# The inverses of the triangular matrices of a gated delta rule, taken in 64x64 diagonal blocks for two heads at a time

## The reference

```python
def gated_delta_rule(q, k, v, g, beta):
    C = DN_CHUNK
    ...
    decay = jnp.where(causal, jnp.exp(jnp.where(causal, diff, 0.0)), 0.0)
    kb = k * beta[..., None]
    L = jnp.where(strict, jnp.einsum('bhnid,bhnjd->bhnij', kb, k) * decay, 0.0)
    u = lax.linalg.triangular_solve(L, v * beta[..., None], left_side=True,
                                    lower=True, unit_diagonal=True)
    ...
    def step(state, inp):
        qd, kd, u_c, w_c, a_c, gl = inp
        v_new = u_c - jnp.einsum('bhcd,bhde->bhce', w_c, state)
        o = (jnp.einsum('bhcd,bhde->bhce', qd, state)
             + jnp.einsum('bhij,bhje->bhie', a_c, v_new))
        state = state * jnp.exp(gl)[..., None, None] + jnp.einsum('bhcd,bhce->bhde', kd, v_new)
        return state, o
```

## Time and profile before

| | us |
|---|---|
| median of 3 runs | 2665.02 (2660.94 to 2666.0) |
| the profiled execution | 2666.18 |
| its span | 2664.4 |
| PE busy | 2563.9 (96%) |
| DVE, ACT, POOL busy | 1277.0, 1043.9, 1094.7 |

### The profile page before, as it was taken

The page is one execution under the profiler, slowest core; times in us unless marked ns, Lnnn a source line. Parts: engine busy times, 40 slices in busy tenths (PEclk is TensorE's granted clock), DMA queues, the critical chain, the costliest instruction groups (busy, mean ns, idle before and its releaser), DMA issues. The chain is left out here.

```text
span 2664.4 us, 32892 instructions
## 1 busy us (share of the span) xinstructions
PE 2563.9 (96%) x12968; PEld 2094.5 (79%) x12968; DVE 1277.0 (48%) x2116; ACT 1043.9 (39%) x2201; POOL 1094.7 (41%) x815
## 2 busy tenths in 40 slices
PE   7999999999999999999999999999988999899998
PEld 6788887778778888778888877787766788777886
DVE  4667764663341111247777546623375311466453
ACT  5464543443343223254555334433431332323332
POOL 2323223224546555433323232256453555244454
PEclk9999999999999999989999999999998999789999
DMA  3111112112222222121111111123132322272222
GB/s 126 63 48 56 48 40 72 48 55 75 93 71 95 93 91 93 63 87 50 56 48 57 40 64 50 54 87 104 63 105 91 105 95 95 68 210 95 87 95 79
DMA packets 76506, 207.64 MB, mean 78 GB/s; under 512 B 16704, under 2 KB 27712, under 8 KB 75712
## 3 DMA queue, kind: packets, MB, share of 16 engines
q1 hardware_dynamic: 76352, 205.53, 22.7%
HBM read 195.01 MB, written 10.49 MB: 77 GB/s over the span
## 5 line engine op out<-in xcount | busy, mean ns | idle before, releaser
L804 POOL TENSOR_TENSOR wL<-raw,wH 128x512 fp32r<-128x512 f32 x672 | 911.0, 1377 | 1317.4 <-ACT wH L797 1317.0
L822 PE MATMUL ps<-hH,wH 128*128 128x512 f32 (+1 forms) x1664 | 698.2, 420 | 16.2 <-DVE rstdp L1540 4.8
L797 ACT ACTIVATE wH<-raw 128x512 fp32r<-128x512 f32 x672 | 386.8, 624 | 805.2 <-PE ps L824 797.6
L823 PE MATMUL ps<-hL,wH 128*128 128x512 f32 (+1 forms) x1664 | 663.9, 399 | 0.0
L824 PE MATMUL ps<-hH,wL 128*128 128x512 f32 (+1 forms) x1664 | 663.5, 399 | 0.0
L822 PEld LDWEIGHTS ps<-hH,wH 128*128 128x128 f32 (+1 forms) x1664 | 315.2, 189 | 92.3 <-issue 30.6
L824 PEld LDWEIGHTS ps<-hH,wL 128*128 128x128 f32 (+1 forms) x1664 | 314.3, 189 | 78.9 <-issue 2.2
L823 PEld LDWEIGHTS ps<-hL,wH 128*128 128x128 f32 (+1 forms) x1664 | 315.8, 190 | 62.5 <-issue 3.1
L822 PE MATMUL ps<-OH,wH 128*128 128x512 f32 x576 | 235.2, 408 | 7.1 <-issue 4.3
L824 PE MATMUL ps<-OH,wL 128*128 128x512 f32 x576 | 228.8, 397 | 0.0
L823 PE MATMUL ps<-OL,wH 128*128 128x512 f32 x576 | 228.8, 397 | 0.0
(11 more groups left out here) (376 smaller groups left out, 3605.8 us busy)
## 6 DMA issues: line engine op xcount, KB each, us to landing
raw<-w SPq DMA_DIRECT2D x345, 512.0 KB, 3.2
mats<-matsD SPq DMA_DIRECT2D x4, 1408.0 KB, 6.5
x<-xT SPq DMA_DIRECT2D x8, 256.0 KB, 7.8
matsD<-Cd SPq DMA_DIRECT2D x8, 256.0 KB, 2.5
matsD<-wide SPq DMA_DIRECT2D x4, 512.0 KB, 3.5
mats<-lagsD SPq DMA_DIRECT2D x32, 64.0 KB, 6.1
outT<-acc SPq DMA_DIRECT2D x8, 256.0 KB, 2.2
cst<-consts SPq DMA_DIRECT2D x1, 1035.0 KB, 6.8
```

The costliest lines, as they stand in the source:

```text
L797: act.activation(weights_at(slot)[0][:, k, :], raw[:, j % RAW, k, :], ACT.Copy).then_inc(high_done, 1)
L804: pool.tensor_tensor(low[:, k, :], raw[:, j % RAW, k, :], high[:, k, :].bitcast(F32), ALU.subtract).then_inc(low_done, 1)
L822: pe.matmul(out, wh, rH[:, t, :], start=(t == 0), stop=False)
L823: pe.matmul(out, wh, rL[:, t, :], start=False, stop=False)
```

## The change

The inverse is now taken for the two 64x64 diagonal blocks of each chunk, with five levels (b = 2 to 32), and for two heads at a time: `A_GROUPS` is (0, 1), (2, 3), (4, 5), (6), (7). The blocks stand side by side in `XB`, upper and lower 64 partitions holding one block each, 256 columns a head. Every `p` and `q` goes chunk by chunk first to the quarter of PE that has rows 0 to 63 and columns 0 to 63 and then to the one that has rows and columns 64 to 127. Both write into the same PSUM bank, to different partitions. The quarter of the full inverse that couples the two blocks comes from a last step: `turn`, `copy`, `plast`, `copylast`, `qlast`, `negate`. Its three PE stages use one quarter each. `copy` also moves both blocks into `XT` (four ACT instructions for a pair), which D no longer writes.

`LTm` has three buffers. `masked` waits for B of head h-3 and for the group of head h-3. The wait for B of head i-4 moves from tile q to tile k. The constants shrink by 448 columns. A memset of a part of `XT` stands ahead of DVE's first wait in each layer. The table of costs is adapted.

```diff
-LEVELS = (2, 4, 8, 16, 32, 64)
+LEVELS = (2, 4, 8, 16, 32)
+BLK = 64
+A_GROUPS = [(0, 1), (2, 3), (4, 5), (6,), (7,)]
+GROUP_OF = {h: g for g, heads in enumerate(A_GROUPS) for h in heads}
...
-for _name, _n in [("ident", P), ("ones", P), ("upper", P), ("first", P), ("later", P), ("levels", P * len(LEVELS)), ("rot", P),
+for _name, _n in [("ident", P), ("ones", P), ("upper", P), ("first", BLK), ("later", P), ("levels", BLK * len(LEVELS)), ("unit", BLK), ("rot", P),
...
+A_STAGES = (["flipi"] + [f"{s}{v}" for v in range(len(LEVELS))
+                         for s in ["p", "pmask", "q", "update"] + (["flip"] if v < len(LEVELS) - 1 else [])]
+            + ["turn", "copy", "plast", "copylast", "qlast", "negate"])
...
-                if i >= 4:
-                    out.append(last("B", i - 4))
+            if k == "k" and s == "tap3" and i >= 4:
+                out.append(last("B", i - 4))
...
             if s == "masked" and j >= 2:
-                out.append(last("A", j - 2))
                 if j >= 3:
-                    out.append(last("B", j - 3))
+                    out += [last("B", j - 3), last("A", GROUP_OF[j - 3])]
         if kind == "A" and s == "flipi":
-            out.append(last("D", j))
+            out.append(last("D", A_GROUPS[j][-1]))
+        if kind == "A" and s == "copy" and A_GROUPS[j][-1] >= 3:
+            out.append(last("B", A_GROUPS[j][-1] - 3))
         if kind == "B" and s == "v0":
-            out.append(last("A", j))
+            out.append(last("A", GROUP_OF[j]))
...
+                        elif kind == "A" and s == "copy":
+                            heads = A_GROUPS[j]
+                            n = len(heads) * CH
+                            if heads[-1] >= 3:
+                                act.wait_ge(scan_stage, B.end(heads[-1] - 3))
+                            act.wait_ge(inverse_stage, A.before(j, "turn"))
+                            for h in heads:
+                                for b in (lower, upper):
+                                    act.activation(XT[b, h % 3, :, b], XB[b, h % 4, :, :], ACT.Copy)
                             act.wait_ge(inverse_stage, A.before(j, s))
+                            act.activation(Xi[lower, 0:n, :], blocks(psA, 0, heads)[lower], ACT.Copy).then_inc(inverse_stage, 1)
...
                             elif s == "first":
-                                ins = v.tensor_tensor(xt, lt, over_chunks(k_("first")), ALU.mult)
+                                for b in (lower, upper):
+                                    ins = v.tensor_tensor(XB[b, h % 4, :, :], lt[b, :, b], over_chunks(k_("first")[b], CH, BLK), ALU.mult)
                             else:
-                                ins = v.tensor_tensor(xt, over_chunks(k_("ident")), xt, ALU.subtract)
+                                ins = v.tensor_tensor(XB[:, h % 4, :, :], over_chunks(k_("unit")), XB[:, h % 4, :, :], ALU.subtract)
...
+                            if s == "negate":
+                                for i, h in enumerate(heads):
+                                    ins = v.tensor_scalar(XT[lower, h % 3, :, upper], blocks(psA, 1, heads)[lower, i * CH:(i + 1) * CH], -1.0, None,
+                                                          ALU.mult)
...
+                            for i in range(len(A_GROUPS[j]) * CH):
+                                c, lt = i % CH, LTm[A_GROUPS[j][i // CH] % 3]
+                                cc = slice(i * BLK, (i + 1) * BLK)
+                                if s == "turn":
+                                    ins = pe.transpose(psA[lower, 0, cc], xb[lower, i, :], ident[lower, lower])
+                                elif s == "plast":
+                                    ins = pe.matmul(psA[upper, 0, cc], lt[lower, c, upper], Xi[lower, i, :], start=True, stop=True)
+                                elif s == "qlast":
+                                    ins = pe.matmul(psA[lower, 1, cc], Pm[upper, i, :], xb[upper, i, :], start=True, stop=True)
                                 else:
+                                    for b in (lower, upper):
+                                        if s[0] == "p":
+                                            ins = pe.matmul(psA[b, 0, cc], lt[b, c, b], Xi[b, i, :], start=True, stop=True)
+                                        else:
+
+                                            n = LEVELS[int(s[-1])]
+                                            ins = pe.matmul(second_half(psA[b, 1, cc], n), Pm[b, i, :], second_half(xb[b, i, :], n),
+                                                            start=True, stop=True)
```

More of the change, by code:

```diff
@@ L259 @@
 G = Count([(0, G_STAGES)])
-A = Count([(h, A_STAGES) for h in range(HEADS)])
+A = Count([(g, A_STAGES) for g in range(len(A_GROUPS))])
 B = Count([(h, B_STAGES) for h in range(HEADS)])
@@ L314 @@
         ("pe", "D", "sums rows gram turnkv"), ("act", "D", "square ksum root exps copykv"), ("pool", "D", "qdec"),
-        ("pe", "A", "p q turn"), ("act", "A", "copy"),
+        ("pe", "A", "p q turn plast qlast"), ("act", "A", "copy copylast"),
         ("pe", "B", "v o r kv turno"), ("act", "B", "copyv osq square root high"), ("pool", "B", "low"),
@@ L747, in second_half, with over_chunks, blocks, of_group @@
             return m.rearrange("p (b n) -> p b n", n=2 * s)[:, :, s:]
-        def over_chunks(m):
-            return m.unsqueeze(1).to_broadcast([P, CH, P])
+        def over_chunks(m, n=CH, rows=P):
+            return m.unsqueeze(1).to_broadcast([rows, n, BLK])
+        lower, upper = slice(0, BLK), slice(BLK, 2 * BLK)
+        def blocks(m, bank, heads):
+            return m[:, bank, 0:len(heads) * CH * BLK].rearrange("p (c n) -> p c n", n=BLK)
+        def of_group(heads):
+            return XB[:, heads[0] % 4:heads[0] % 4 + len(heads), :, :].rearrange("p h c n -> p (h c) n")
         names = ("loaded0", "loaded1", "loaded2", "high_done", "low_done", "tile_done", "tile_stage",
@@ L1369, in _ @@
                 def _(v):
+                    v.memset(XT[upper, :, :, lower], 0.0)
                     v.wait_ge(params_in, 16)
@@ L1441, in _ @@
                             ins.then_inc(gram_stage, 1)
-                        elif kind == "A" and s[:-1] in ("pmask", "update", "flip"):
+                        elif kind == "A" and (s[:-1] in ("pmask", "update", "flip") or s == "negate"):
+                            heads = A_GROUPS[j]
+                            n = len(heads) * CH
                             if s == "flipi":
-                                v.wait_ge(gram_stage, D.end(j))
+                                v.wait_ge(gram_stage, D.end(heads[-1]))
@@ L1450, in _ @@
                             elif s.startswith("pmask"):
                                 lev = int(s[-1])
-                                m = k_("levels")[:, lev * P:(lev + 1) * P]
-                                ins = v.tensor_tensor(Pm[:, :, :], chunks(psA[:, 0, :]), over_chunks(m), ALU.mult)
+                                m = k_("levels")[:, lev * BLK:(lev + 1) * BLK]
+                                ins = v.tensor_tensor(Pm[:, 0:n, :], blocks(psA, 0, heads), over_chunks(m, n), ALU.mult)
@@ L1693, in _ @@
                             ins.then_inc(gram_stage, 1)
[L1694 to L1702, removed]
-                                else:
-                                    b = LEVELS[int(s[-1])]
-                                    ins = pe.matmul(second_half(psA[:, 1, cc], b), Pm[:, c, :], second_half(XT[:, h % 3, c, :], b),
-                                                    start=True, stop=True)
+                        elif kind == "A" and (s[:-1] in ("p", "q") or s in ("turn", "plast", "qlast")):
+                            pe.wait_ge(inverse_stage, A.before(j, s))
+                            xb = of_group(A_GROUPS[j])
+                            for i in range(len(A_GROUPS[j]) * CH):
[7 more added lines that the diff above has]
+                                    ins = pe.matmul(psA[lower, 1, cc], Pm[upper, i, :], xb[upper, i, :], start=True, stop=True)
+                                else:
+                                    for b in (lower, upper):
[5 more added lines that the diff above has]
+                                                            start=True, stop=True)
```

45 lines of the change are left out of this document (24 added, 21 removed), and 2 rows, old and new, of the table special.

## The result

The changed kernel takes 2754.7 us (median of four runs) against 2665.4: the ratio is 1.034, 95% interval 1.0319 to 1.0361. It is slower by 89 us, where 2629 was forecast. From the page of the kernel after: the span, the engines, and the slices of PE and of its clock, as in the earlier trace rows.

The account below looks back on a forecast made before the run. PE was taken to set the pace in both layers' head stretches. From the profiled 2666.2 us, less 42.6 of PE work and 1 for constants, plus 8 idle, came 2630.6, or 2629 as median; range 2600 to 2678.

Parts of the forecast that it names:

- Prices of the small matmuls: PE's p and q stages: 0.034 us a matmul, 1.31 a pair stage with entry and exit, 0.76 a single; last step 0.06.
- DVE's work to `ga` 0: DVE in the head stretch: flip, mask and update run once per pair, removing 45 of 252 us, less 3 for `negate`.
- D behind `masked`, 5 us: In the loop of pairs: only the end of D, from `masked` on, follows B of an earlier head, 5 us a round.
- the prediction's own sum: Serial chain of A, B and D over layer 0's heads, from D of head 1 at 117 to B of head 7 at 433.
- The gate and its margin of 24 us: First stage of tile `ga` 0 waits for B of head 7, with 24 us to spare before the change, used up after.
- PE's saving of 42.6 us: PE's work on the inverse: 67.3 us a layer against 88.6, so 21.3 less a layer, 42.6 in all.
- 8 us of idle: PE idle time where the loop of pairs and the stream of tiles meet: 4 us a layer, between 0 and 36.
- The loop of pairs decides: Rival: with loaded durations B of head 7 ends at 469, 32 us more a layer than allowed: 2693; chance 0.12.
- The quarters don't overlap: Rival: a matmul in PE's quarter stages costs 0.056, a pair's stage 2.00 us, total 2684; chance 0.11.
- The clock falls: Rival: PE's granted clock drops in the head stretches, eight falls of 5 us a layer, 40 us: 2669; chance 0.04.
- All comes back: Rival: no PE idle time and free entries into the small stages, 2608; chance 0.13.

## Why the prediction was wrong

In the order of its steps, with layer 0's numbers.

**Prices of the small matmuls: right.** A pair stage's 32 matmuls take 1.08 us (1.10 taken), entry 0.32 for 0.33, sixteen of a single head 0.61 (0.55 taken; 150.37 to 150.98 above). The last step was 1.07 us for 16 (169.38 to 170.45 in the last fence below), 0.067 each, where 0.06 was taken. The single heads show most of the sum as time, with one of three tables: 22 us won, where these prices give 27 for eight singles. DVE's work to `ga` 0 fell from 263.0 to 227.4, 36 us where 42 was forecast.

**The loop's term "D behind `masked`, 5 us": the step that failed.** The wait for B of head h-3 stands at three places of D: at `masked`, at `qdec` on POOL and, much earlier, at `qscale`, its first stage on DVE. The list of conditions ahead of the prediction has `masked` alone, and the prediction read the last place. In the kernel before, `qscale` of D 3 starts at 182.9, 12 us after B 0, and of D 7 at 347.5, 16 after B 4, so this wait was met when it came and no row of waits shows it; only the code does. With the pairs it isn't met, and nearly all of D comes behind B: 26, 26 and 23 us in the three rounds of a layer, not 5. With 26 put into the prediction's own sum, up to D 7:

117 + 42 + 33 + 26 + 42 + 33 + 26 + 42 + 33 + 26 = 420.

Measured: 423.4. The other terms were off in ways that cancel: D 1 ended at 127.0, not 117 (the levels of A 0 left PE, but D 1 isn't earlier for it; why isn't settled), A took 46 to 50 instead of 42, B 25 or 26 instead of 33. The kernel with the later wait shows some 10 us a round of the term by itself. It doesn't bring all back, since 13 to 15 us of D stay behind B.

**The gate and its margin of 24 us: wrong too, and independently.** The prediction took `ga` 0 to follow B 7 with 24 us to spare. It stood 24 us behind B 7 before and stands 24 behind it now (480.6 and 504.4), which looks like a gate and isn't one: with D's later wait it comes 14.7 us behind B 7 (458.2 and 472.9). Like `scale` of tile `swq` 0, `rotk` of tile `swk` waits for D 7, which the list ahead of the prediction leaves out. `swv` and the eight `swq` lie between `swk` and `ga` 0. In the fourteen kernels, before and after among them, `ga` 0 comes 77.7 to 83.8 us after D 7 ended, while D 7's end itself goes from 359.4 to 496.0. Before, `rotk` of `swk` ran 0.7 us after the end of D 7 (374.42 and 373.70), and PE was full from there on. So there was no margin against D 7 in the stream of tiles: 423.35 + 81.08 = 504.43. From 420 the prediction's sum would have said 500. Against 453.9 that is 46 a layer, 92 in all, less 1 at the start: 2756 for the median, where 2754.7 was measured. The part that agrees so well is partly luck, by the terms that cancel.

**PE's saving of 42.6 us: right as work, worth nothing as time.** With the chain in charge, 21 us less work a layer is only 21 us more idle. The prediction added the saving to the sum and 8 us of idle beside it, when the loop should have been asked first.

**The rivals.** "The loop of pairs decides" was the mechanism, with D 7 for B 7 as its last member and the price of D left out: 2693 for 2754.7. "The quarters don't overlap": refuted. (The 0.66 us that spoke against it is a row's own length, to be set beside 1.06 and not 0.90; that makes the argument stronger.) "The clock falls": it does, to 0.91 over the stretch, but in the old arithmetic under pair waits as well (0.88), so that the small stages aren't needed for it. How much of A's 47 us is due to it stays open. "All comes back", 2608: no kernel came near it; the best, with all heads single, took 2643.5.

**What was read wrongly.** Full PE and idle 5 us of 380 say that PE sets the pace of this order of work. They don't say how long the serial chain is that would take over, and the margins of that chain were 11 to 16 us at `qscale` of heads 3 to 7 and none at D 7.

## What to carry to other kernels

Before joining two units of a pipelined serial chain into one, write down all waits between its stages, the met ones too, at the first place where each stands, and add the chain up from release to release; an engine at 99% doesn't show how near it is. Cut the work per unit first without joining: here the smaller blocks gave 22 us at best by themselves, and the pairing lost 111. Before a gain of some 20 us is put down to the arithmetic, plan the order from more than one table. A gate is found by a distance that stays the same over kernels that move it, with the engine full in between, not by the event that happens to stand before it.

## What the runs showed of the chip

Two diagonal quarters of the array, fed in turn, do 0.034 us a matmul (float32 in two parts, 64 x 64 weights, 64 columns) and 0.057 when fed one after the other; it is the order of the instructions that gives the overlap, 1.7 times.

The granted clock can fall while PE has no idle time: from 130 to 173 us PE was busy without a gap, and the clock was 1.00 from 150 to 173 and 0.50 from 174 to 175. Timeline of PE in the changed kernel, a `plast` of sixteen matmuls on one quarter and eight matmuls of one column, then a `qlast`, also on one quarter, and the tile behind it:

```profile
169.38 1.14 PE L1739 MATMUL ps<-Xi,LTm 64*64 64x64 f32 x16
170.45 1.05 PE L1719 MATMUL ps<-cst,sq 128*128 128x1 f32 x8
...
172.23 1.14 PE L1741 MATMUL ps<-XB,Pm 64*64 64x64 f32 x16
173.30 0.74 PE L838 MATMUL ps<-hH,wH 128*128 128x512 f32 x1
173.84 0.63 PE L839 MATMUL ps<-hL,wH 128*128 128x512 f32 x1
174.27 0.63 PE L840 MATMUL ps<-hH,wL 128*128 128x512 f32 x1
...
170.00:175.00 5.00, 5.00 (x40) 4.17 (x39) 2.21 (x5) 2.35 (x4) 1.89 (x2) 0.84 0.01 3
```

The last row is the window: PE busy for 5.00 of 5.00 us, clock 0.84. A matmul of a tile has its successor after 0.43 us here (173.84 to 174.27) instead of 0.23, nearly twice as long: the lower of the two levels, 1.2 GHz. What stood before the fall were stages on one quarter and of one column. The stretch with all heads single has such stages as well, half as long each, and ran at 1.00, so they don't bring it about by themselves.
